# Every second pair of the first feed-forward product, and three gate pairs, as seven block products between down products

## What is computed

```python
for i in range(DEPTH):                       # DEPTH = 2
    m = hybrid_mixer(...) if i % 2 == 0 else mla_mixer(...)
    h = layer_norm(DN_ALPHA * x + m, ln1_g[i], ln1_b[i])
    f = jnp.square(jax.nn.relu(h @ mlp_w1[i])) @ mlp_w2[i]        # 1024 -> 4096 -> 1024
    e = jax.nn.sigmoid(h @ ple_w_gate[i]) * (p[i] @ ple_w_proj[i])
    x = layer_norm(DN_ALPHA * h + f + e, ln2_g[i], ln2_b[i])
```

## Time and profile before

| | |
|---|---|
| Median of 3 runs | 2369.64 us (2368.81 to 2370.12) |
| Profiled execution | 2369.66 us, its span 2367.9 us |
| TensorE busy | 2241.0 us, 95% of the span |
| VectorE, GpSimd, ScalarE busy | 767.2, 605.6, 423.3 us |
| Granted TensorE clock | 0.99 of the full 2.4 GHz |

### The profile page before, as it was taken

The page is one execution under the profiler, slowest core; times in us unless marked ns, Lnnn a source line. Parts: engine busy times, 40 slices in busy tenths (PEclk is TensorE's granted clock), DMA queues, the critical chain, the costliest instruction groups (busy, mean ns, idle before and its releaser), DMA issues.

```text
span 2367.9 us, 31852 instructions
## 1 busy us (share of the span) xinstructions
PE 2241.0 (95%) x13790; PEld 1521.5 (64%) x13790; DVE 767.2 (32%) x1343; ACT 423.3 (18%) x887; POOL 605.6 (26%) x507
## 2 busy tenths in 40 slices
PE   9999999999999999999988888899999999888888
PEld 8776676686668899998333333278999863333333
DVE  5533224524216755643100000055755221000001
ACT  3311112621103331221000000033112120000001
POOL 2377732258762045510000000011545000000000
PEclk9999999999999999999999999999999999999999
DMA  7277732348752442349999999953333799999997
GB/s 278 102 310 289 297 133 97 130 186 338 297 216 76 145 141 93 108 179 398 428 428 428 427 427 428 417 212 112 124 120 125 287 408 428 428 428 426 428 426 314
DMA packets 136855, 654.82 MB, mean 277 GB/s; under 512 B 9864, under 2 KB 15112, under 8 KB 108168
## 3 DMA queue, kind: packets, MB, share of 16 engines
q1 hardware_dynamic: 136712, 652.72, 69.1%
HBM read 651.64 MB, written 1.05 MB: 276 GB/s over the span
## 4 chain that ended last, share of the span: by engine, by line
PE 74%; DMA 20%; DVE 3%; ACT 1%; issue 1%; SPq 1%; POOL 0%; DVEq 0%; ACTq 0%; POOLq 0%
PE bank L823 73%; DMA ring<-in_w_exp_up 10%; DMA PRGT<-in_w_exp_up 5%; DMA PRGT<-in_w_exp_down 3%; DMA PRGT<-in_w_exp_gate 1%; ACT R L3423 1%; SPq L737 1%; PE bank L1453 0%; DVE sm L2199 0%; POOL PRGT L3521 0%; ACT SQ L3463 0%; PE bank L1009 0%; DVE PRGT L2677 0%; DVE PRGT L2193 0%; DVE PRGT L2682 0%
## 5 line engine op out<-in xcount | busy, mean ns | idle before, releaser
L823 PE MATMUL bank<-hT,ring 128*128 128x256 f32 (+1 forms) x2736 | 541.4, 355 | 0.0
L823 PEld LDWEIGHTS bank<-hT,ring 128*128 128x128 f32 x2736 | 469.6, 190 | 70.3 <-issue 15.3
L823 PE MATMUL bank<-PRGT,R 128*32 128x512 f32 (+1 forms) x1248 | 290.7, 576 | 29.1 <-DMA PRGT<-in_w_exp_up 18.5
L823 PE MATMUL bank<-ring,R 128*32 128x512 f32 (+1 forms) x992 | 252.4, 591 | 36.7 <-DMA ring<-in_w_exp_up 21.6
L3638 POOL TENSOR_TENSOR SQ<-xT 128x512 f32<-128x512 f32 x4 | 4.2, 1057 | 1051.2 <-DVE xT L2960 1051.0
L823 PE MATMUL bank<-PRGT,ring 128*128 128x256 f32 (+6 forms) x1440 | 238.4, 353 | 0.4 <-ACT PRGT L3166 0.4
L823 PEld LDWEIGHTS bank<-PRGT,ring 128*128 128x128 f32 (+3 forms) x1440 | 200.0, 176 | 32.5 <-issue 3.0
L823 PEld LDWEIGHTS bank<-PRGT,R 128*32 128x32 f32 (+1 forms) x1248 | 88.4, 120 | 192.5 <-issue 191.9
L823 PE MATMUL bank<-PRGT,SQ 128*32 128x512 f32 (+2 forms) x864 | 193.1, 530 | 13.7 <-ACT SQ L3463 12.2
L823 PEld LDWEIGHTS bank<-ring,R 128*32 128x32 f32 (+1 forms) x992 | 70.6, 115 | 165.5 <-issue 164.8
L823 PE MATMUL bank<-ring,SQ 128*32 128x512 f32 (+2 forms) x640 | 167.3, 519 | 8.3 <-ACT SQ L3463 8.3
(11 more groups left out here) (430 smaller groups left out, 2668.2 us busy)
## 6 DMA issues: line engine op xcount, KB each, us to landing
PRGT<-in_w_exp_gate SPq DMA_DIRECT2D x42, 2048.0 KB, 31.9
ring<-in_w_exp_up SPq DMA_DIRECT2D x36, 2048.0 KB, 31.9
ring<-in_mlp_w SPq DMA_DIRECT2D x32, 2048.0 KB, 9.5
PRGT<-in_w_exp_down SPq DMA_DIRECT2D x30, 2048.0 KB, 31.4
PRGT<-in_w_exp_up SPq DMA_DIRECT2D x28, 2048.0 KB, 31.9
PRGT<-in_w_ada SPq DMA_DIRECT2D x32, 1536.0 KB, 11.9
ring<-in_w_exp_down SPq DMA_DIRECT2D x24, 2048.0 KB, 33.5
ring<-in_w_exp_gate SPq DMA_DIRECT2D x22, 2048.0 KB, 31.9
```

What stands on the lines that cost most here:

```text
L823: return mm(o, lhsT=lhsT, rhs=rhs, start=first, stop=last, **kw)
```

## The change

In both layers, the pairs q = 2, 4, ..., 14 of `hidden` and gate pairs 0, 1 and 2 are done in seven block products too: 28 matmuls of 128 x 128 (56 records) in the place of 16 of 128 x 256 (32 records). `hidden_and_down(q)` sets the blocks of an up pair between the products of down(q-1). Three of the seven end in the same corner of the bank, one after the other, and ScalarE copies each out (`corners_out`) before the next is written. DVE makes the sums of the hidden state once a layer (`hidden_sums`), four sums of the weights for each such pair (`column_sums`, 128 x 512 each), and joins the result from bank and copies (`ff_joined`, three operations); for up pairs ScalarE's Relu then reads that joined tile. The loop of the ada steps is written out, and its steps are set among the new operations by the table `first`. The gate pairs' joins come ahead of L2278 (0 and 1) and within the loop of L2287 (2). One semaphore, `c_sig`, is folded into another.

```diff
+UP_SEVEN = (2, 4, 6, 8, 10, 12, 14)
+GATE_SEVEN = (0, 1, 2)
...
+        FF_HSUM = [k4(flat(t)) for t in (hsum3.rearrange("p (a s) -> p a s", a=2), POOL_CD[:, 78:80, :], SQ[:, 4:6, :], SQ[:, 6:8, :])]
+        UP_WS = [k4(flat(R[:, 2 * r:2 * r + 2, :])) for r in range(3)]
+        UP_CORNERS = flat(R[:, 6:8, :])[:, 0:384]
...
+                def block_product(dst, lhs, rhs, first=False):
+                    for k in range(4):
+                        ins = mul(dst, lhs[:, k, :], rhs[:, k, :], first and k == 0, False, skip_group_check=True)
+                    return ins
+                def hidden_and_down(q):
+                    j, s, sums, at = q % 2, slots[2 * (q % 4 // 2)][0], ff_sums_at(l, q=q), 3 * ff_seven_at(l, q=q)
+                    s1, s2, s4 = UP_WS
+                    t1, t2, t3, t4 = FF_HSUM
+                    z, y1, w, y = regions(ff_bank(l))
+                    if j == 0:
+                        pe.wait_ge(slot_full[s], loaded(slots[2 * (q % 4 // 2)][1], q // 4))
+                    pe.wait_ge(sems["ff_read"], FF_PAIRS * l + q)
+                    block_product(z, column_block(s, j, 0, 0), h_block(0, 0), True).then_inc(sems["corner_full"], 1)
+                    down(q - 1, 0, 1)
+                    pe.wait_ge(sems["sums_ready"], sums + 2)
+                    pe.wait_ge(sems["corner_read"], at + 1)
+                    block_product(z, s2, t2).then_inc(sems["corner_full"], 1)
+                    down(q - 1, 1, 2)
+                    pe.wait_ge(sems["sums_ready"], sums + 4)
+                    pe.wait_ge(sems["corner_read"], at + 2)
+                    block_product(z, column_block(s, j, 0, 1), t3).then_inc(sems["corner_full"], 1)
+                    down(q - 1, 2, 3)
+                    pe.wait_ge(sems["corner_read"], at + 3)
+                    block_product(z, column_block(s, j, 1, 0), h_block(1, 0), True)
+                    block_product(y, s1, t1)
+                    block_product(w, column_block(s, j, 1, 1), t4)
+                    block_product(y1, s4, h_block(1, 1)).then_inc(sems["ff_full"], 1)
+                    down(q - 1, 3, 7)
...
+                    z, y1, w, y = regions(bk(n))
+                    x = bk(n + 1)[:, 0:P]
+                    pe.wait_ge(bank_read[n % BANKS], emptied(n))
+                    pe.wait_ge(sems["sums_ready"], sums + 1)
+                    block_product(z, column_block(s, j, 1, 0), h_block(1, 0), True)
+                    pe.wait_ge(sems["combined"], 8 * l + 1 + r)
+                    block_product(x, column_block(s, j, 0, 0), h_block(0, 0), True).then_inc(sems["corner_full"], 1)
+                    block_product(y, s1, t1)
+                    pe.wait_ge(sems["sums_ready"], sums + 2)
+                    pe.wait_ge(sems["corner_read"], at + 1)
+                    block_product(x, s2, t2).then_inc(sems["corner_full"], 1)
+                    block_product(w, column_block(s, j, 1, 1), t4)
+                    pe.wait_ge(sems["sums_ready"], sums + 4)
+                    pe.wait_ge(sems["corner_read"], at + 2)
+                    block_product(x, column_block(s, j, 0, 1), t3).then_inc(sems["corner_full"], 1)
+                    block_product(y1, s4, h_block(1, 1)).then_inc(bank_full[n % BANKS], 1)
...
-                def down(q):
+                def down(q, r0=0, r1=7):
...
-                    for o, lhs, rhs in zip(corners(l), (a11, a12, s4, a22, s1, s2, s3), (b11, b21, b22, t4, t1, t2, t3)):
+                    products = tuple(zip(corners(l), (a11, a12, s4, a22, s1, s2, s3), (b11, b21, b22, t4, t1, t2, t3)))
+                    for o, lhs, rhs in products[r0:r1]:
                         ins = mul(o[:, :], lhs, rhs, q == 0, q == FF_PAIRS - 1, skip_group_check=True)
-                    ins.then_inc(sems["down_done"], 1)
+                    if r1 == 7:
+                        ins.then_inc(sems["down_done"], 1)
...
+                    if q in UP_SEVEN:
+                        hidden_and_down(q)
+                        continue
...
+            def column_sums(n, s, j, ws):
+                s1, s2, s4 = ws
+                a11, a12, a21, a22 = (column_block(s, j, kb, h) for h in range(2) for kb in range(2))
+                added(n + 1, v.tensor_tensor(s1, a21, a22, ALU.add))
+                added(n + 2, v.tensor_tensor(s2, s1, a11, ALU.subtract))
+                added(n + 3, v.tensor_tensor(s4, a12, s2, ALU.subtract))
+                added(n + 4, v.tensor_tensor(a21, a11, a21, ALU.subtract))
...
+            def ff_joined(f0, f1, c, o):
+                v.tensor_tensor(f0, c[:, 0:2 * P], o[:, 0:2 * P], ALU.add)
+                v.tensor_tensor(two(f1), bcast(c[:, 2 * P:3 * P], 2), two(o[:, 2 * P:4 * P]), ALU.add).then_inc(sems["vec_chain"], 1)
+                dve.wait_ge(sems["vec_chain"], L.up())
+                return v.tensor_tensor(f0[:, P:2 * P], f0[:, P:2 * P], o[:, 3 * P:4 * P], ALU.add)
+            def up_joined(l, q):
+                dve.wait_ge(sems["ff_full"], FF_PAIRS * l + q + 1)
+                dve.wait_ge(sems["corner_read"], 3 * ff_seven_at(l, q=q) + 3)
+                t = 2 * (q % 4)
+                ff_joined(FF[:, t, :], FF[:, t + 1, :], UP_CORNERS, ff_bank(l)).then_inc(sems["ff_read"], 1)
...
-                ada(l)
+                if UP_SEVEN or GATE_SEVEN:
+                    hidden_sums(l)
+                first = {1: (0,), 2: (1, 2), 3: (3, 4), 4: (5,), 5: (6, 7)}
+                for q in range(1, FF_PAIRS):
+                    steps = first.get(q, (q + 2,) if q + 2 < 2 * KT else ())
+                    early = 1 < q < 6
+                    if early:
+                        ada(l, steps[0])
+                    if q in UP_SEVEN:
+                        up_joined(l, q)
+                    if q + 1 in UP_SEVEN:
+                        up_sums(l, q + 1)
+                    for i in steps[early:]:
+                        ada(l, i)
+                    if q == FF_PAIRS - 2:
+                        for j in GATE_SEVEN[:2]:
+                            gate_sums(l, j)
+                    if q == FF_PAIRS - 1:
+                        for j in GATE_SEVEN[2:]:
+                            gate_sums(l, j)
...
                 combine(c22, CORNER, p5)
+                for j in GATE_SEVEN[:2]:
+                    gate_joined(l, j)
                 dve.wait_ge(sems["down_turned"], L.nxt("down_turned", 4))
...
+                    if j in GATE_SEVEN[2:]:
+                        gate_joined(l, j)
...
+            def corners_out(o, c, at):
+                for r in range(3):
+                    act.wait_ge(sems["corner_full"], 3 * at + r + 1)
+                    f(c[:, r * P:(r + 1) * P], o[:, 0:P], ACT.Copy).then_inc(sems["corner_read"], 1)
...
+                    if q in UP_SEVEN:
+                        corners_out(ff_bank(l), UP_CORNERS, ff_seven_at(l, q=q))
+                        act.wait_ge(sems["ff_read"], FF_PAIRS * l + q + 1)
+                        f(tile_, tile_, ACT.Relu).then_inc(sems["ff_chain"], 1)
+                        act.wait_ge(sems["ff_chain"], ff_seven_at(l, q=q) + 1)
+                    else:
+                        act.wait_ge(sems["ff_full"], FF_PAIRS * l + q + 1)
+                        f(tile_, ff_bank(l)[:, :], ACT.Relu).then_inc(sems["ff_read"], 1)
+                        act.wait_ge(sems["ff_read"], FF_PAIRS * l + q + 1)
                     f(tile_, tile_, ACT.Square).then_inc(sems["ff_act"], 1)
...
+                    if j in GATE_SEVEN:
+                        corners_out(bk(n + 1), ple_corners(j), ff_seven_at(l, j=j))
+                        act.wait_ge(bank_read[n % BANKS], filled(n))
+                        t = flat(SQ[:, 2 * j:2 * j + 2, :])
+                        f(t, t, ACT.Sigmoid).then_inc(sems["ff_chain"], 1)
+                        return
```

More of the change, by code:

```diff
@@ L240, in nxt, with ff_seven_at, ff_sums_at, corner_at @@
         return self.seen[name]
+UP_SEVEN = (2, 4, 6, 8, 10, 12, 14)
+GATE_SEVEN = (0, 1, 2)
+FF_SEVEN = len(UP_SEVEN) + len(GATE_SEVEN)
+def ff_seven_at(l, q=None, j=None):
+    return FF_SEVEN * l + (UP_SEVEN.index(q) if j is None else len(UP_SEVEN) + GATE_SEVEN.index(j))
+def ff_sums_at(l, q=None, j=None):
+    first = 4 * (FF_SEVEN + 1) * l
+    return first if q is None and j is None else first + 4 * (ff_seven_at(l, q, j) - FF_SEVEN * l + 1)
+FF_SUMS, FF_CORNERS = 4 * (FF_SEVEN + 1) * DEPTH, 3 * FF_SEVEN * DEPTH
+def corner_at(l, p):
+    return FF_CORNERS + 2 * seven_at(l, p)
 def seven_at(l, p):
@@ L515, in corner_copies, with gate_ws, ple_corners, column_block @@
             return CORNERS[SEVEN.index(p) % 2]
+        FF_HSUM = [k4(flat(t)) for t in (hsum3.rearrange("p (a s) -> p a s", a=2), POOL_CD[:, 78:80, :], SQ[:, 4:6, :], SQ[:, 6:8, :])]
+        UP_WS = [k4(flat(R[:, 2 * r:2 * r + 2, :])) for r in range(3)]
+        UP_CORNERS = flat(R[:, 6:8, :])[:, 0:384]
+        def gate_ws(j):
+            return [k4(flat(PR[:, 6 * j + 2 * r:6 * j + 2 * r + 2, :])) for r in range(3)]
+        def ple_corners(j):
```

(21 more changed lines are left out.)

59 lines of the change are left out of this document (43 added, 16 removed).

## The result

The changed kernel takes 2378.43 us (median of 7 runs, 2377.01 to 2380.63), the kernel before 2369.68 (2368.81 to 2370.12): a ratio of 1.0037, 95% interval 1.0027 to 1.0046. It is 8.7 us slower; the prediction was 2376.4, slower by 6.7. Three of its terms were right, one did not occur in the profiled execution, and one was missing; the two errors nearly cancel, which is luck.

The account below looks back on a forecast made before the run. TensorE, busy 95% of the span, was taken to bound the kernel. Against 2369.66 us, -12.9 + 8.6 + 5.0 + 6.0 = +6.7 gave 2376.4 us, with a range from 2362 to 2390.

Parts of the forecast that it names:

- The saving: Up and gate pairs, both layers: seven products save 0.645 us a pair, 20 pairs, -12.9 us if TensorE never waits.
- The covers: Feed-forward stages: corner copies, joins and hidden-state sums lie behind other work, all priced at nothing.
- Pair 4: Up pair 4, each layer: TensorE waits 4.3 us for POOL's row sums of pair 3; two layers +8.6 us.
- Gate pair 2: Gate pair 2, each layer: the fourth block waits 3.0 us for a corner copy behind ScalarE's square; two layers +6.0.
- Pair 6: Up pair 6, each layer: ada steps and new sums delay POOL's row sums, 0 to 3.9 us, taken as 2.5.
- step 7 will only in part fall into the window: Before up pair 6: ada step 7 only partly overlaps the time for POOL's row sums, hence 2.5 us a layer.
- The later pairs: Up pairs from 8 on: one ada step a pair, eight possible stalls of 0 to 2.6 us, taken as 0.
- The weight loads: Rival for the seven-product pairs: weight loads lie bare, so nothing is saved; near 2448 us, chance 0.01.
- the second rival: Feed-forward stages: only up pair 4 and the gates wait, +1.7 us, 2371.4, no change to be told; chance 0.22.

Follow-up runs that it names:

- both repairs: Changed kernel with the row-sum wait moved to down product 2 and gate pair 2's copies ahead of the square on ScalarE: 2357.88 us, ratio 0.9952.
- up pairs only: Changed kernel with the up pairs alone as seven products, no gate pair: 2373.64 us, ratio 1.0013.
- the wait filled: Changed kernel with pair 4's first block product done five times and gate pair 2's corner product three times, nothing released earlier: 2378.24 us.

## Why the prediction was right, and where it was not

**The saving** (-12.9): right. In the kernel after, pair 2 runs from 145.01 to 157.28, 12.27 us against 12.92, and the kernel with both repairs shows the sum.

**The covers**: right. But for the copies of gate pair 2, which were priced apart, TensorE waits for no corner copy and no join in any trace, and the second block of gate pair 0 follows the first. The sums of the hidden state did meet POOL's work (1.7 us each for three of them, not 0.69), which no one waited for.

**Pair 4** (4.3 forecast, 4.1 measured): the mechanism and its steps were right. The timelines of DVE and of POOL after, which answer and the earlier trace rows:

```profile
155.03 6.94 DVE L2353 SCALAR_TENSOR_TENSOR PRGT<-PRGT,sm 128x3072 f32<-128x3072 f32 x2
163.41 1.71 DVE L2374 TENSOR_TENSOR R<-ring 128x512 f32<-128x512 f32 x1 [1.44 <-DMA ring<-in_mlp_w]
...
170.18 3.49 DVE L2353 SCALAR_TENSOR_TENSOR PRGT<-PRGT,sm 128x3072 f32<-128x3072 f32 x1
```

```profile
156.59 2.17 POOL L3751 TENSOR_TENSOR SQ<-PRGT 128x128 f32<-128x128 f32 x1 [4.30 <-ACT PRGT L3327]
158.83 3.45 POOL L3752 TENSOR_TENSOR SQ<-SQ,PRGT 128x128 f32<-128x128 f32 x1
...
164.65 1.60 POOL L3742 TENSOR_TENSOR ring<-ring 128x512 f32<-128x512 f32 x1
...
170.54 3.45 POOL L3752 TENSOR_TENSOR SQ<-SQ,PRGT 128x128 f32<-128x128 f32 x1
...
174.60 0.45 POOL L3754 TENSOR_TENSOR SQ<-PRGT 128x128 f32<-128x128 f32 x1
```

Steps 2 and 3 run back to back from 155.03, the row sums of pair 2 are held by both, each sum of DVE's costs POOL 0.33 (1.60 for 1.27; forecast 0.26), and step 4 holds the second row sum of pair 3 for 3.00 (3.45 for 0.45; forecast 2.99). The row sums end at 175.05 (forecast 175.4).

**Gate pair 2** (3.0 forecast, 2.8 measured): right; ScalarE's copy began 0.53 us behind the square's start and not 0.63 (353.07 to 353.60).

**Pair 6** (+2.5 a layer): wrong in the profiled execution, which waits nothing there, and a matter of tenths of a microsecond in others. The step that failed is "step 7 will only in part fall into the window", priced at 2.5 us. In the rows here a POOL operation that begins during an ada step is held until the step ends (2.17 us for 0.45 at 156.59 above, from the middle of a step; 3.45 when it meets a whole one), and one that has begun before the step is not. So whether the row sums are held at all hangs on which begins first. The timelines of DVE and POOL in the kernel after:

```profile
201.28 3.50 DVE L2353 SCALAR_TENSOR_TENSOR PRGT<-PRGT,sm 128x3072 f32<-128x3072 f32 x1 [7.02 <-DMA PRGT<-in_w_ada]
...
201.12 0.45 POOL L3754 TENSOR_TENSOR SQ<-PRGT 128x128 f32<-128x128 f32 x1
```

and in the kernel with the copies ahead of the square, with PE:

```profile
199.64 3.42 DVE L2353 SCALAR_TENSOR_TENSOR PRGT<-PRGT,sm 128x3072 f32<-128x3072 f32 x1 [6.64 <-DMA PRGT<-in_w_ada]
...
199.85 3.53 POOL L3757 TENSOR_TENSOR SQ<-PRGT 128x128 f32<-128x128 f32 x1
...
203.52 1.10 PE L865 MATMUL bank<-ring,PRGT 128*128 128x512 f32 x2 [1.40 <-POOL SQ L3757]
```

In the first, step 7 began 0.16 us after POOL's last row sum had begun (in layer 1 0.68 us after), and nobody waited; in the second 0.21 us ahead of it, and TensorE waited 1.40 us. The waits of 1.52 us (up pairs only) and 2.67 us (the wait filled) in layer 0 have the same cause. That this makes the changed kernel's times spread more (3.6 us against 1.3) fits, but was only argued.

**The later pairs** (0): right, no wait for the row sums from pair 8 on in any trace. **The weight loads** as a rival: a block product is 0.89 us in the up pairs too, loads included.

**The missing term.** I priced a wait at its length. Here, in the kernel after, each of the four waits costs 1.7 to 2.8 us more behind it: 8.9 us in the profile after (2.83 and 1.70 in layer 0; in layer 1, worked out in the same way, 2.68 and 1.70). With the four waits as measured, 13.8 us, the sum is -12.9 + 13.8 + 8.9 = +9.8, and TensorE is 9.6 late behind both layers after a start 0.2 early. Without this term it would have been +0.9, no change to be told. The forecast's +6.7 held because pair 6's 5.0 stood in the place of the 8.9. That is luck: the waits that came are those of the second rival (pair 4 and the gate pairs only, 2371.4), and a term that was not in the sum brought the time up to the forecast.

The trace of the kernel before had this term in view. Two rows of its timeline of PE, in the mixture of experts, have the same count and shape behind a wait of the same length:

```profile
1174.95 8.61 PE L823 MATMUL bank<-ring,R 128*32 128x512 f32 x32 [2.73 <-DMA ring<-in_w_exp_up]
...
1233.68 7.06 PE L823 MATMUL bank<-PRGT,R 128*32 128x512 f32 x32 [2.73 <-DMA PRGT<-in_w_exp_up]
```

Behind the first the granted clock is 0.50 from 1174.7 to 1178.0 us, and the row is 1.55 us longer; behind the second the clock stays at 1.00.

## What to carry to other kernels

Find the first reader of what a wait guards: here two of the seven down products didn't need the row sums, and moving the wait past them, and three copies past one square, turned a change that lost 8.7 us into one that gains 11.9. Price a stall of a busy TensorE at its length and what the clock takes behind it. Where two engines hold each other up for the length of an operation, as DVE and POOL do here, a long operation moved out of one window can land in the next (pair 6 waited 7.0 us): work out the next window before the edit is made.

## What the runs showed of the hardware

In the feed-forward stages of the nine changed kernels' traces, the granted clock fell behind each of ten waits of TensorE of 3.6 us and longer, behind six of nine of 2.63 to 2.67 us, and behind none of those of 0.38 to 1.52 us, whose next blocks keep 0.89 us. In the kernel after, layer 0, its mean is 0.55 in the 6.5 us behind pair 4's wait and 0.61 in the 4.4 us behind gate pair 2's. The kernel with ada step 4 later has two of the three exceptions, one in each layer:

```profile
358.16 1.13 PE L865 MATMUL bank<-PRGT 128*128 128x128 f32 x8 [2.63 <-ACT PRGT L3302]
359.12 1.95 PE L865 MATMUL bank<-SQ,ring 128*128 128x128 f32 x16
```

Short waits are not safe everywhere: at the start of the second mixer, behind two of 0.99 and 0.65 us, the clock fell in two of the traces (22.24 and 22.30 us in the place of 20.91). The price differed for the same wait: 2.83 us behind one of 3.95 us, and 1.7 behind those of 3.96 in both layers of the kernel with the copies ahead of the square. The Trainium skill, "TensorE: Matmul & The Clock Gate", section "What's actually happening", says that the slower level is the default and that activity of the engine releases it; these rows and the fill run agree. What decides whether a given wait of some 2.6 us is followed by a fall was not found out.
